# A diffusion layer on one core: nine adaLN weight tiles multiplied in two rounded passes instead of plain fp32

## The reference

```python
ml = jnp.split((jax.nn.silu(c) @ ada_w[i] + ada_b[i])[:, None, :], N_MOD, axis=-1)
mc = jnp.split((jax.nn.silu(c_ctx) @ ada_w[i] + ada_b[i])[None, None, :], N_MOD, axis=-1)
x = ffn_sublayer(x, ml[0], ml[1], ml[2], ffn1_norm[i], ...)
# ffn_sublayer: h = rms_norm(t, norm_g) * (1 + scale) + shift
#               t + gate * 0.5 * (silu(h @ w_gate) * (h @ w_up)) @ w_down
```

## Time and profile before

| | |
|---|---|
| timed runs | 1467.06, 1464.08, 1467.01 us; median 1467.01 |
| profiled execution | 1463.88 us; span of its instructions 1462.2 us |
| TensorE busy | 1431.8 us, 98% of the span; mean granted clock 0.990 |
| VectorE, ScalarE, GpSimd busy | 695.0, 266.0 and 664.9 us |
| chain that ended last | PE 93%, DVE 3%, ACT 2% of the span |
| first matmul of the SwiGLU | 53.76 us after the start of the span |

### The profile page before, as it was taken

How to read it: one execution, slowest core, us unless ns; L and a number is a source line. 1 busy time by engine, 2 the same in 40 slices (tenths; PEclk the granted TensorE clock), 3 DMA queues, 4 the chain that set the end, 5 groups by cost and what they waited for, 6 DMA issues and landing times.

```text
span 1462.2 us, 19104 instructions
## 1 busy us (share of the span) xinstructions
PE 1431.8 (98%) x7912; PEld 1253.2 (86%) x7912; DVE 695.0 (48%) x1032; ACT 266.0 (18%) x440; POOL 664.9 (45%) x389
## 2 busy tenths in 40 slices
PE   7999999999999999999999999999999999999997
PEld 3699999999999999987888888888898888888886
DVE  2774467467455455246436449615775112112114
ACT  3320010010010010023534321124131000000104
POOL 1363443433443433433600456624739657566661
PEclk9999999999999999999999999999999999999998
DMA  9532354353353343123210277384646333233321
GB/s 350 158 108 63 117 146 117 103 146 103 117 146 104 116 133 104 43 49 115 87 30 1 57 193 224 104 258 156 203 132 187 97 91 101 87 101 101 94 66 58
DMA packets 232563, 174.31 MB, mean 119 GB/s; under 512 B 28664, under 2 KB 212124, under 8 KB 232476
## 3 DMA queue, kind: packets, MB, share of 16 engines
q1 hardware_dynamic: 213296, 142.50, 33.4%
q10 hardware_dynamic: 19180, 30.58, 6.5%
HBM read 155.26 MB, written 17.79 MB: 118 GB/s over the span
## 4 chain that ended last, share of the span: by engine, by line
PE 93%; DVE 3%; ACT 2%; issue 1%; DMA 1%; SPq 0%; DVEq 0%; ACTq 0%
PE ps L888 58%; PE ps L1143 15%; PE ps L1146 4%; PE ps L897 2%; PE ps L920 2%; PE ps L1241 2%; PE ps L1095 1%; PE ps L985 1%; PE ps L1050 1%; PE ps L976 1%; PE ps L1397 1%; PE ps L1351 1%; PE ps L1355 1%; DMA x_in<-in_ctx_dram 1%; PE ps L1433 1%
## 5 line engine op out<-in xcount | busy, mean ns | idle before, releaser
L818 POOL TENSOR_SCALAR w_hi<-w_raw 128x1024 fp32r<-128x1024 f32 (+1 forms) x187 | 212.3, 1135 | 746.9 <-issue 456.9
L821 POOL TENSOR_TENSOR w_lo<-w_raw,w_hi 128x1024 fp32r<-128x1024 f32 (+1 forms) x187 | 451.2, 2413 | 15.6
L888 PE MATMUL ps<-h_hi,w_lo 128*128 128x384 f32 (+1 forms) x1224 | 381.1, 360 | 0.0
L888 PE MATMUL ps<-h_hi,w_hi 128*128 128x384 f32 (+1 forms) x1224 | 378.3, 358 | 0.0
L888 PE MATMUL ps<-h_lo,w_hi 128*128 128x384 f32 (+1 forms) x1224 | 378.3, 358 | 0.0
L888 PEld LDWEIGHTS ps<-h_hi,w_lo 128*128 128x128 f32 x1224 | 221.7, 189 | 23.6 <-issue 2.5
L888 PEld LDWEIGHTS ps<-h_hi,w_hi 128*128 128x128 f32 x1224 | 223.8, 189 | 20.4
L888 PEld LDWEIGHTS ps<-h_lo,w_hi 128*128 128x128 f32 x1224 | 223.6, 189 | 20.2
L2200 DVE SCALAR_TENSOR_TENSOR ps<-ps,silu 128x768 f32<-128x768 f32 (+1 forms) x44 | 36.5, 831 | 253.3 <-PE ps L888 247.1
L2230 DVE SCALAR_TENSOR_TENSOR x<-ps,mod,x 128x512 f32<-128x512 f32 x88 | 64.8, 749 | 168.3 <-PE ps L1146 90.8
L1143 PE MATMUL ps<-act_hi,w_lo 128*128 128x512 f32 x336 | 133.8, 398 | 1.8 <-DVEq L2205 1.8
(11 more groups left out here) (374 smaller groups left out, 1869.8 us busy)
## 6 DMA issues: line engine op xcount, KB each, us to landing
w_raw<-in_ffn_w_gate_dram SPq DMA_DIRECT2D x44, 512.0 KB, 3.9
w_raw<-in_ffn_w_up_dram SPq DMA_DIRECT2D x44, 512.0 KB, 3.9
w_raw<-in_ffn_w_down_dram SPq DMA_DIRECT2D x40, 512.0 KB, 3.6
ada_w<-in_ada_w_dram ACTq DMA_DIRECT2D x32, 512.0 KB, 4.0
w_raw<-in_w_in_dram SPq DMA_DIRECT2D x32, 512.0 KB, 4.1
ada_w<-in_ada_w_dram SPq DMA_DIRECT2D x30, 512.0 KB, 4.8
c_scr<-cp ACTq DMA_DIRECT2D x16, 288.0 KB, 3.7
b_scr<-bt_sb ACTq DMA_DIRECT2D x16, 256.0 KB, 4.0
```

The source lines that it names most:

```text
L818: pool.tensor_scalar(w_hi[:, s, 0:cols], w_raw[:, s, 0:cols], 1.0, 1.0, ALU.mult, ALU.mult)\
L821: pool.tensor_tensor(w_lo[:, s, 0:cols], w_raw[:, s, 0:cols], w_hi[:, s, 0:cols].bitcast(F32), ALU.subtract).then_inc(w_split, 1)
L888: last = pe.matmul(mv[2], st, mv[part], start=(first and q == 0), stop=(n == len(terms) - 1 and q == 2))
```

## The change

Blocks 1 and 0 are still multiplied on PE, but nine of their sixteen tiles (block 1: k = 2 to 7, block 0: k = 0 to 2; the list `STACKED`) are split first: ACT rounds a tile into a ring of six, `tile_hi` (`round_tile`), and DVE writes the rest over the loaded tile (`low_tile`, places by `first_low`). PE then makes two fp32r passes over each, one over the rounded part, one over the rest, each against four stationary columns, `cs_parts`: the rounded conditioning (two columns, made by ACT) and its rest (two, by DVE). The row in PSUM so has four lines; the other seven tiles are multiplied plainly, with `cs` widened by two columns of zeros. The four lines are turned together, and the two halves are added in the bias step, which has two instructions now (`quad_bias`).

What moves with it: job `lam` with its turn goes from behind `row1` to behind the turn of block 0, and `s5_lambda` on DVE from ahead of `col1` to between the fourth and fifth `h_lo`. POOL waits for `cols_ok` in place of job `row1` before it splits the first four units. SP issues the first gate unit behind tiles 0 to 3 of block 0 and the first up unit behind tiles 4 to 7.

```diff
+STACKED = [(1, k) for k in range(2, 8)] + [(0, 0), (0, 1), (0, 2)]
+HI_RING = 6
...
-_number(JOB, [("vec", 1), ("x", KD), ("row1", 1), ("lam", 1), ("spread", 1), ("col1", 1), ("row0", 1), ("col0", 1), ("skip", 1),
+_number(JOB, [("vec", 1), ("x", KD), ("row1", 1), ("spread", 1), ("col1", 1), ("row0", 1), ("col0", 1), ("lam", 1), ("skip", 1),
...
             for n in range(2):
-                sp.dma_start(raw(n, KD, P), first_src[n][:, :, 0:P]).then_inc(w_here[n], 16)
                 for k in range(4 * n, 4 * n + 4):
                     sp.dma_start(first_tile(0, k), ada_src(0, k)).then_inc(ada_here0[0][k], 16)
+                sp.dma_start(raw(n, KD, P), first_src[n][:, :, 0:P]).then_inc(w_here[n], 16)
...
                         if fresh and n < 4:
-                            is_done(pool, JOB["row1"])
+                            pool.wait_ge(cols_ok, 1)
...
                 for k in range(KD):
-                    pe.wait_ge(ada_here0[g][k], 16)
-                    for q in range(2):
-                        last = pe.matmul((lat, ctx_)[q](j)[0:2, :], cs[:, k, :], first_tile(g, k)[:, 512 * q:512 * q + 512],
-                                         start=(k == 0), stop=(k == KD - 1))
+                    if (g, k) in STACKED:
+                        n = STACKED.index((g, k))
+                        pe.wait_ge(cs_lo_ok, 1)
+                        pe.wait_ge(tile_lo_ok, n + 1)
+                        passes = [(cs_parts, tile_hi[:, n % HI_RING, :]), (cs_parts, first_low(g, k))]
+                    else:
+                        pe.wait_ge(ada_here0[g][k], 16)
+                        passes = [(cs, first_tile(g, k))]
+                    for r, (st, mv) in enumerate(passes):
+                        if r:
+                            last.then_inc(tile_used, 1)
+                        for q in range(2):
+                            last = pe.matmul((lat, ctx_)[q](j)[0:4, :], st[:, k, :], mv[:, 512 * q:512 * q + 512],
+                                             start=(k == 0 and r == 0), stop=(k == KD - 1 and r == len(passes) - 1))
...
             ins.then_inc(silu_c, 1)
+            act.wait_ge(silu_c, 1)
+            act.activation(cs_parts[:, :, 0:2], cs[:, :, 0:2], ACT.Copy).then_inc(cs_hi_ok, 1)
...
+            def round_tile(n):
+
+                g, k = STACKED[n]
+                act.wait_ge(ada_here0[g][k], 16)
+                if n >= HI_RING:
+                    act.wait_ge(tile_used, n - HI_RING + 1)
+                act.activation(tile_hi[:, n % HI_RING, :], first_tile(g, k), ACT.Copy).then_inc(tile_hi_ok, 1)
+
+            is_done(act, JOB["x"] + KD - 1)
+            act.wait_ge(ms_ok, 6)
+            for n in range(HI_RING):
+                round_tile(n)
             j = JOB["row1"]
             is_done(act, j)
...
             act.sem_inc(row_ok, 1)
+            for n in range(HI_RING, len(STACKED)):
+                round_tile(n)
...
+            def quad_bias(quads, g):
+
+                t = slice(KD * g, KD * g + KD)
+                link(TT(mod[:, t, :], quads[:, :, 0:2], vt[:, t].unsqueeze(2).to_broadcast([P, KD, 2]), ALU.add))
+                link(TT(mod[:, t, :], mod[:, t, :], quads[:, :, 2:4], ALU.add))
...
+            dve.wait_ge(cs_hi_ok, 1)
+            TT(cs_parts[:, :, 2:4], cs[:, :, 0:2], cs_parts[:, :, 0:2].bitcast(F32), ALU.subtract).then_inc(cs_lo_ok, 1)
             dve.wait_ge(root_ok, 1)
             dve.reciprocal(root[:, :], root[:, :]).then_inc(root_inv, 1)
-            s5_lambda()
+
+            def low_tile(n):
+
+                g, k = STACKED[n]
+                dve.wait_ge(tile_hi_ok, n + 1)
+                TT(first_low(g, k), first_tile(g, k), tile_hi[:, n % HI_RING, :].bitcast(F32),
+                   ALU.subtract).then_inc(tile_lo_ok, 1)
+
+            for n in range(len(STACKED)):
+                low_tile(n)
...
                 ins.then_inc(h_ok, 1)
+                if k == 3:
+                    s5_lambda()
```

More of the change, by code:

```diff
@@ L280, in build @@
     amul = place("amul", [P, 3, KD, 2], F32)
-    cs = place("cs", [P, KD, 2], F32)
+    cs = place("cs", [P, KD, 4], F32)
+    cs_parts = place("cs_parts", [P, KD, 4], F32R)
     eps = place("eps", [P, 1], F32)
@@ L383, in build @@
     scaled = place("scaled", [P, KD, NT], F32, at=scratch_at)
-    ada_row = place("ada_row", [2, 2, D], F32, at=ada_at + 4 * ADA_RING * D)
+    ada_row = place("ada_row", [4, 2, D], F32, at=ada_at + 4 * ADA_RING * D)
+    tile_hi = place("tile_hi", [P, HI_RING, D], F32R, at=h_at)
+    ada_w0_low = place("ada_w0_low", [P, ADA_RING0, D], F32R, at=h_at + 24 * KB)
+    ada_last_low = place("ada_last_low", [P, KD - ADA_RING0, D], F32R, at=scratch_at + 24 * KB)
     assert scratch_at + 32 * KB <= s5_at
@@ L391, in first_tile, with first_low @@
         return ada_w0[:, k, :] if k < ADA_RING0 else ada_last[:, k - ADA_RING0, :]
+    def first_low(g, k):
+        if g:
+            return (w_hi, w_lo)[k // ADA_EARLY][:, k % ADA_EARLY, :]
+        return ada_w0_low[:, k, :] if k < ADA_RING0 else ada_last_low[:, k - ADA_RING0, :]
     s5p = [s5_at]
@@ L452, in ada_cols, with ada_quads @@
         return lat(j)[:, c0:c0 + 2 * KD].rearrange("p (t v) -> p t v", v=2)
+    def ada_quads(j):
+        return lat(j)[:, 0:4 * KD].rearrange("p (t v) -> p t v", v=4)
     def ada_vec(g, v):
@@ L505, in build @@
         row_half_ok = sem("row_half_ok")
+        cs_hi_ok = sem("cs_hi_ok")
+        cs_lo_ok = sem("cs_lo_ok")
+        cs_zero = sem("cs_zero")
+        tile_used = sem("tile_used")
+        tile_hi_ok = sem("tile_hi_ok")
+        tile_lo_ok = sem("tile_lo_ok")
         acc_ok = sem("acc_ok")
@@ L930, in turn_row @@
                         pe.wait_ge(row_half_ok, 1)
-                    last = transpose(ada_cols(j)[:, t, :], ada_row[:, g, P * t:P * t + P])
+                    last = transpose(ada_quads(j)[:, t, :], ada_row[:, g, P * t:P * t + P])
                 last.then_inc(job_done, count)
             pe.wait_ge(silu_c, 1)
+            pe.wait_ge(cs_zero, 1)
             row_products(1)
-            j = JOB["lam"]
-            pe.wait_ge(small_in, 16 * SMALL)
-            wait_read(pe, j)
-            transpose(lat(j)[:, 0:DG], lam_in[:, 0, :])
-            transpose(lat(j)[:, P:P + 4], gn_in[:, :])
-            transpose(lat(j)[:, DG:2 * DG], lam_in[:, 1, :]).then_inc(job_done, 1)
             j = JOB["spread"]
@@ L955, in _ @@
             pe.wait_ge(row_ok, 2)
-            turn_row(0, 2)
+            turn_row(0, 1)
+            j = JOB["lam"]
+            pe.wait_ge(small_in, 16 * SMALL)
+            wait_read(pe, j)
+            transpose(lat(j)[:, 0:DG], lam_in[:, 0, :])
+            transpose(lat(j)[:, P:P + 4], gn_in[:, :])
+            transpose(lat(j)[:, DG:2 * DG], lam_in[:, 1, :]).then_inc(job_done, 2)
             def s5_side(i, v, j):
@@ L1565, in _ @@
             act.activation(root[:, :], root[:, :], ACT.Sqrt, bias=eps[:, :], scale=1.0 / D).then_inc(root_ok, 1)
+            def round_tile(n):
[8 more added lines that the diff above has]
+                round_tile(n)
             j = JOB["row1"]
             is_done(act, j)
-            act.activation(ada_row[:, 1, :].rearrange("p (b c) -> p b c", b=2), both(j, 512)[0:2], ACT.Copy)\
+            act.activation(ada_row[:, 1, :].rearrange("p (b c) -> p b c", b=2), both(j, 512)[0:4], ACT.Copy)\
                 .then_inc(slot_read[j % 4], 1)
@@ L1672, in _ @@
                 ins.then_inc(h_hi_ok, 1)
+            act.wait_ge(small_in, 16 * SMALL)
             act.activation(s5t[:, 1, :], s5t[:, 0, :], ACT.Exp).then_inc(s5_act, 1)
@@ L2361, in _ @@
             dve.wait_ge(xn_ok, KD)
-            dve.sem_inc(slot_read[JOB["spread"] % 4], 2)
+            dve.sem_inc(slot_read[JOB["spread"] % 4], 1)
             j = JOB["row0"]
             is_done(dve, j)
-            dve.tensor_copy(ada_row[:, 0, 512:D], ctx_(j)[0:2, :]).then_inc(row_half_ok, 1)
+            dve.tensor_copy(ada_row[:, 0, 512:D], ctx_(j)[0:4, :]).then_inc(row_half_ok, 1)
             dve.wait_ge(row_half_ok, 1)
@@ L2370, in _ @@
             is_done(dve, j)
-            ada_bias(ada_cols(j), 0).then_inc(shift_ok, 1)
-            dve.wait_ge(shift_ok, 1)
+            quad_bias(ada_quads(j), 0)
+            dve.sem_inc(shift_ok, 1)
             dve.sem_inc(slot_read[j % 4], 1)
```

7 lines of the change are left out of this document (4 added, 3 removed).

## The result

The changed kernel takes **1467.93 us**, the median of 20 runs (1465.72 to 1470.53), beside 1464.22 for the kernel before in the same measurement (20 runs, 1461.92 to 1467.06). The ratio is 1.0021, with a 95% interval of 1.0015 to 1.0027: 3.1 us slower by the ratio (2.2 to 4.0), just past the 0.2% that the prediction took for the least a measurement can tell, where 2.4 us faster were forecast. Its profiled execution took 1467.74 us with a span of 1465.9; that of before took 1463.88 with 1462.2.

What follows compares the result with a forecast made beforehand. TensorE bounds the opening up to the first SwiGLU; 4.6 us won there, cut to 2.4 by h_lo's wait for GpSimd, gives 1463.88 - 2.4 = 1461.5, or 1464.6 from the median; predicted midway 1463.0, range 1459 to 1466.

Steps and rivals of the forecast that it cites:

- the part on the clock: Half clock after the SwiGLU's start costs 1.5 us as before; everything behind that start just shifts, 2.4 us earlier.
- rival 3: Clock falls to 1.2 GHz through row 0's five plain tiles; SwiGLU at 57.8, 1467.9 us, 4 us slower; chance 0.07.
- Two passes: Nine adaLN tiles: 0.92 us each instead of 1.73, but paced by VectorE at 1.2; row 1 done at 29.4.
- Row 0: Shift columns before the SwiGLU: third stacked tile finished at 36.15, five plain ones taking 8.65 us, done at 44.8.
- The scale columns and GpSimd: `cols_ok` at 35.9; GpSimd's split of four weight units, waiting for it, runs from 36.1 to 50.1.
- The lock: Port shared by VectorE and GpSimd: first h_lo waits until 50.1, SwiGLU starts at 51.4, gain 2.4 us instead of 4.6.
- Rival 1: GpSimd does not get in h_lo's way; SwiGLU starts at 49.2, time 1459.3 us; chance 0.2.
- rival 2: VectorE's nine subtractions cost 1.58 us a tile, adding 3.4; SwiGLU at 54.8, 1464.9 us; chance 0.15 with its milder form.
- The late load: Up weights, moved behind all eight adaLN tiles, arrive late: nothing taken, at worst 1 us; start 52.4, 1462.5 us.
- The clock behind the gap: TensorE idle from 46.6 to 51.4; half clock afterwards costs 1.5 us as before, bounds 1.5 better or worse.
- Rival 4: An fp32r pass with four stationary columns runs at fp32 rate, 3.46 us per tile; slower by over 10 us; chance 0.01.
- The tests named: Signs in the changed profile's opening; wrong if h_lo is short and begins before 50, or TensorE's clock under 1.00 before 46.

Runs made afterwards that it cites:

- b_192: The kernel before with 192 unused bytes ahead of act_hi, nothing else; 1469.78 us, ratio 1.0022.
- a_512: The changed kernel with 320 unused bytes, so act_hi and all behind it lie 512 bytes behind their old place; 1463.99 us, ratio 0.9983 to the kernel before.
- a_256: The changed kernel with 64 unused bytes, so act_hi lies 256 bytes behind its old place; 1464.65 us, ratio 0.9985 to the kernel before.
- c_early: a_512 with ScalarE rounding the last three tiles ahead of its copy of row 1 too; 1461.28 us, ratio 0.9971 to the kernel before.
- e_best: a_512 with all nine tiles rounded before row 1's copy and 11 needless matmuls in the gap before the SwiGLU; 1461.71 us, ratio 0.9967.
- c_late: a_512 with GpSimd's third and fourth units held back until all h_lo is made; 1464.99 us, ratio 0.9997 to the kernel before.
- c_fill: a_512 with 14 needless fp32 matmuls behind the lambda turn, where TensorE is idle; 1459.35 us, ratio 0.9962 to the kernel before.
- d_last: a_512 with only GpSimd's fourth unit held back until all h_lo is made; 1466.58 us, ratio 0.9997 to the kernel before.

## Why the prediction was wrong, step by step

- **The step that failed** is the last sentence of the part on the clock: "Behind the SwiGLU's start nothing else is touched, and all of it shifts." Nothing there is executed otherwise, but 192 bytes that two small tiles take slow some 760 passes by 0.006 us each; less what the 256-column passes of `m` gain, that is 3.8 us by the traces. b_192 has the whole effect and a_512 is rid of it. The shift was put at all of 2.4 us. The opening in fact brought 1.3 us at the end of the joint units, and 1.3 less 3.8 is 2.5 us slower, within the measured 2.2 to 4.0. None of the four rivals had it. The trace of before holds no second placement to compare with, so no row of it could have priced this; a look at where tiles land would have shown that something behind the opening did move.
- **Luck:** rival 3's time, 1467.9, is the measured one to the first decimal. That is chance. It asked for a half clock over all five plain tiles of row 0 and a SwiGLU that starts at 57.8; the clock was 1.00 there and the start at 50.41.
- **Two passes:** predicted one tile every 1.2 us, paced by VectorE; measured 1.13. VectorE's first six subtractions ran from 20.73 to 27.64 (forecast 21.3 to 28.5), and row 1 was done at 28.88 (forecast 29.4). Right. (Four passes at 0.225 are 0.90, not 0.92; nothing hangs on it, since VectorE sets the pace.)
- **Row 0:** done at 44.8 by the forecast, 45.74 in the changed kernel, 44.90 in a_512. The 32 instructions took 13.19 us in the one and 12.05 in the other (32.85 to 44.90), and the 1.14 between them is the fall of the clock over three tiles. That is **rival 3's mechanism**, near the place named and at 1.14 of its 8.65 us: the five plain tiles ran at 1.00 again. The time didn't lose it: in a_512 and a_256, without that fall, h_lo waits for GpSimd instead, and the SwiGLU starts no earlier (50.69 and 50.77).
- **The scale columns and GpSimd:** GpSimd was to start at 36.1 and end at 50.1; it did at 35.50 and 49.32. The 14 us for four units held.
- **The lock:** the forecast had h_lo stand until GpSimd's end, at 50.1, and the start 1.3 us after it, at 51.4. GpSimd ended at 49.32, 49.60 and 49.68 in the changed kernel, a_512 and a_256, and TensorE started 1.09 us after it in all three. The mechanism was right and its end 0.8 early; as a sum, 2.4 was forecast and 2.5 came. In the changed kernel row 0's slower clock took part of the wait's place: h_lo came up 0.9 us later than forecast and was 0.33 too long, not 2. a_512 shows the wait in full, 2.62 for 1.16. The Trainium skill's rule ("SBUF — State Buffer", SBUF: two separate sides), an exclusive lock, agrees with that row. In c_early and e_best, where both engines have several instructions to run, the stretched durations on both sides fit engines that take turns. Rival 1 is out.
- **VectorE (rival 2):** a subtraction took 1.24 by the row of one, 3.50 for three together. Out. The late load, its milder form, would have had a price of nothing in the changed kernel; c_early shows that it lands at 38.9, just before the 38.95 at which the changed kernel takes it up, and in c_late GpSimd waited 0.29 for it. That cover was thinner than I took it for.
- **The clock behind the gap:** taken the same as before, with a fall twice as long for a bound, 1.5 worse. The fall was 6.8 us where it had been 3.4, and the joint units 1.21 longer. The term was mis-sized; its bound held. The opening's net gain at the end of the joint units, counted from row 1's start, is therefore 1.3 us, not 2.4.
- **Rival 4** (the rate of an fp32r pass with four stationary columns) is out: a tile with two passes over both halves took 1.08 to 1.10.
- **The tests named** read mostly as for a right forecast (nine subtractions of 1.24, GpSimd's end, the first L1132), and the time was wrong all the same. Of those that would have made it wrong the clock under 1.00 before 46 came true, and half of another: h_lo began before 50, and was nearly short (1.49). A test of the end of the program, such as the step of a down projection, was missing.

## What to carry to other kernels

When a change adds or resizes a tile in SBUF, look at what is laid out behind it: compare the start-to-start step of a pass that the change doesn't touch, and keep the distance between streamed and stationary tiles as it was (in this kernel, as a multiple of 256 bytes). Before taking away a wait of one engine for another, list what queues behind the engine that will wait instead. A gain that stands at one landmark is not yet a gain at the end: compare several landmarks along the chain. And compare them in more than one profile of each kernel, since falls of the clock come and go between executions: here one profile of the kernel before hid 1.6 us.

## What was not expected of the hardware

- A 512-column fp32r pass took 0.2269 us with the streamed tile a multiple of 256 bytes from the weight tiles (0, 256, 512), and 0.2287, 0.2325 and 0.2329 at 64, 128 and 192. Moving the tiles together by 128 left it at 0.2268. Where 512- and 256-column passes alternate, no such dependence shows. The cause is open.
- The clock fell to 0.50 behind short gaps too: after 28.90 to 32.60, in which TensorE was busy for 1.93 of 3.70 us, it was 0.50 for 3.40 us in the changed kernel. It was 0.50 there in c_late, c_fill and d_last too, and 1.00 in a_512 and a_256, though the six programs are the same up to there but for the place of tiles. What decides between them the runs don't show.
- A dozen needless matmuls in a gap before dense work paid for themselves: 1.65 us in the kernel before, 1.9 us in a_512, each by one pair of profiles.
